# Differential attention beside products: one group of score matmuls per step, two maps in two row halves

## The reference, cut to what matters

```python
q1, q2 = split(h @ w_q)            # each 8 heads x 64, rms_norm per head
kv = rms_norm(h, kv_norm_g) @ w_kv # k1, k2: 8 heads x 64, rms_norm per head; vb: 8 heads x 128
for each head, for each block of queries:
    a = softmax(mask(q1 @ k1.T * scale + bias)) - lam * softmax(mask(q2 @ k2.T * scale + bias))
    o = a @ vb
o = rms_norm(o, sub_g) * (1.0 - lam_init)
h = h + o @ w_o
```

## Time and profile before

| | |
|---|---|
| median of the runs | 2430.57 us |
| profiled execution | 2428.51 us |
| its span, first to last instruction | 2427.2 us |
| PE busy | 2271.9 us (94%), 19314 records |
| PEld busy | 1959.8 us (81%) |
| DVE / ACT / POOL busy | 1460.1 (60%) / 931.3 (38%) / 456.9 us (19%) |
| mean granted TensorE clock | 0.96 |

### The profile page before, as it was taken

One profiled execution on the slowest core, in us unless ns is written; L12 is line 12 of the kernel. 1 busy time (PEld: TensorE's weight loads), 2 busy tenths in 40 slices (PEclk: granted clock), 3 DMA queues, 4 the chain that ended last, 5 costly groups with the idle time before them and its releaser, 6 DMA issues.

```text
span 2427.2 us, 44082 instructions
## 1 busy us (share of the span) xinstructions
PE 2271.9 (94%) x19314; PEld 1959.8 (81%) x19314; DVE 1460.1 (60%) x2342; ACT 931.3 (38%) x1538; POOL 456.9 (19%) x253
## 2 busy tenths in 40 slices
PE   4898999999969999996999999999999998999999
PEld 1677777777757788775689999999877778999987
DVE  3678888888775524377546767533444445776722
ACT  1324444444332525232544343323445545434321
POOL 0444334334302443422220000000000011000000
PEclk7899999999989999896899999999999999999999
DMA  6541011111225234210012332233210012333232
GB/s 235 130 108 45 11 41 41 41 41 41 71 88 160 87 95 142 70 53 26 1 41 86 92 95 89 88 95 115 64 50 27 18 35 88 91 92 93 86 97 73
DMA packets 56831, 184.70 MB, mean 76 GB/s; under 512 B 6816, under 2 KB 6816, under 8 KB 56640
## 3 DMA queue, kind: packets, MB, share of 16 engines
q1 hardware_dynamic: 56640, 181.89, 24.5%
HBM read 174.99 MB, written 6.88 MB: 75 GB/s over the span
## 4 chain that ended last, share of the span: by engine, by line
PE 76%; DVE 15%; ACT 5%; issue 2%; DMA 1%; POOL 0%; SPq 0%; DVEq 0%; POOLq 0%; ACTq 0%
PE PS L532 59%; PE PS L662 4%; DVE ca L1867 3%; PE PS L1106 2%; PE PS L1137 2%; PE PS L857 1%; PE PS L995 1%; PE PS L918 1%; DVE Swk L2220 1%; DVE kx L1935 1%; DVE mx L2216 1%; PE PS L963 1%; PE PS L551 1%; DVE Bf L1941 1%; ACT La L1184 1%
## 5 line engine op out<-in xcount | busy, mean ns | idle before, releaser
L2545 POOL TENSOR_TENSOR wlo<-raw,whi 128x1024 fp32r<-128x1024 f32 (+1 forms) x130 | 304.2, 2341 | 937.2 <-ACT whi L1184 931.1
L532 PE MATMUL PS<-nhi,whi 128*128 128x264 f32 x2064 | 443.9, 296 | 7.1 <-DVE nlo L2108 6.7
L532 PE MATMUL PS<-nlo,whi 128*128 128x264 f32 x2064 | 423.8, 288 | 0.0
L532 PE MATMUL PS<-nhi,wlo 128*128 128x264 f32 x2064 | 421.6, 286 | 0.3 <-POOL wlo L2545 0.3
L1184 ACT ACTIVATE whi<-raw 128x1024 fp32r<-128x1024 f32 (+2 forms) x298 | 302.2, 1015 | 236.6 <-PE PS L532 208.2
L532 PEld LDWEIGHTS PS<-nhi,whi 128*128 128x128 f32 x2064 | 324.2, 191 | 41.1 <-issue 32.9
L532 PEld LDWEIGHTS PS<-nhi,wlo 128*128 128x128 f32 x2064 | 325.0, 191 | 0.5 <-POOL wlo L2545 0.5
L532 PEld LDWEIGHTS PS<-nlo,whi 128*128 128x128 f32 x2064 | 325.2, 191 | 0.0
L1779 DVE TENSOR_TENSOR wlo<-raw,whi 128x1024 fp32r<-128x1024 f32 (+1 forms) x168 | 201.1, 1197 | 168.1 <-ACT whi L1184 167.8
L532 PE MATMUL PS<-hhi,whi 128*128 128x512 f32 x648 | 264.3, 408 | 6.6 <-DVE hlo L1846 6.6
L532 PE MATMUL PS<-hhi,wlo 128*128 128x512 f32 x648 | 258.5, 399 | 1.4 <-POOL wlo L2545 1.4
(11 more groups left out here) (353 smaller groups left out, 3600.6 us busy)
## 6 DMA issues: line engine op xcount, KB each, us to landing
raw<-in_wall SPq DMA_DIRECT2D x290, 512.0 KB, 3.6
raw<-in_wall SPq DMA_DIRECT2D x16, 384.0 KB, 3.1
TZ<-g_rows SPq DMA_DIRECT2D x2, 2112.0 KB, 8.3
raw<-in_wall SPq DMA_DIRECT2D x16, 256.0 KB, 2.6
g_rows<-gsb SPq DMA_DIRECT2D x8, 328.0 KB
xt<-in_xT SPq DMA_DIRECT2D x1, 2048.0 KB, 13.4
o_rows<-os SPq DMA_DIRECT2D x8, 256.0 KB, 2.2
keep<-o_rows SPq DMA_DIRECT2D x8, 256.0 KB, 4.4
```

The source lines that it names most:

```text
L532: q = e.matmul(out, cuts[a][:, k * P:(k + 1) * P], (hi_, lo_)[b][:, kr, lo:lo + w], start=start and k == 0 and a == b == 0, stop=stop and ...
L2545: e.tensor_tensor(wlo[slot[i]][:, w], raw[i % NRAW][:, w], whi[slot[i]][:, w].bitcast(F32), ALU.subtract).then_inc(*up("lo_pool", i))
```

## The change

Four things, in one edit.

1. **A head's two maps share a tile.** The columns of `w_q` and of the keys' part of `w_kv` are put in another order when the inputs are laid out, so that tile h of `qB` and `kB` holds head h: its first map on partitions 0 to 63, its second on 64 to 127. Units of `b_kv` now come as k, v, k, v. `place` is gone; each head is finished by itself.
2. **Both maps of a step are scored in one place**, piece by piece of 136 (or 72) keys, the two maps in turn and so the two row halves in turn. The 528-wide step still scores its maps apart, but with apply and three product steps between them.
3. **The strings.** 16 g instead of 32 come first; `BESIDE` puts scores, apply and turn of a turn next to each other; `AFTER` now holds g as well, since 16 product steps are left for it.
4. **Copies and order on the other engines.** The last 16 keys go to bank 6 beside the whole tiles (bank 7 for the 528-wide step alone); all copies of an even step are ScalarE's and all of an odd step VectorE's. `apply` waits for the copy `b_o` of the apply before it. VectorE inverts the sums of step n-1 ahead of scores(n); ScalarE's order in a turn is scale(n-1), copy(n-3), exponentials(n), PTb copy(n-2). The last q tile is normalized after the first four roundings of the keys' operand (`n2_hi`) instead of before all eight.

```diff
-BESIDE = "agagagagg" "agagagag" "agagagag" "aagaag" "aaaag"
-AFTER = "ag" * 10
+BESIDE = "aagggaagg" "aaaagggg" "aagaaggg" "aaaagg" "aaaag"
+AFTER = "aaggaagg" "aaaagg" "aaagg" "agg" "aagg" "aagg"
...
-            for name in "g" * 32 + 8 * BESIDE + AFTER:
+            for name in "g" * 16 + 8 * BESIDE + AFTER:
...
+        def rest_at(w):
+            return (6, w // P * P) if w < 512 else (7, 256)
...
-                def scores(n, s):
+                def scores(n, maps):
                     h, i = steps[n]
                     q0, nq, w = rows_of(i)
-                    rows, kt = rowsof[h % 2], 4 * s + h // 2
...
-                    scores_free((4, 5) if w > 512 else (4 + s,), ("b_max", n, s))
-                    for out, lo, m_ in halves(w, 4 if w > 512 else 4 + s):
-                        q = e.matmul(out[0:nq, :], qB[rows, kt, q0:q0 + nq], kB[rows, kt, lo:lo + m_], start=True, stop=True)
-                    q.then_inc(*up("b_scores", n, s))
+                    on.wait_ge(*at("qb", h))
+                    on.wait_ge(*at("kb", h))
+                    wide = w > 512
+                    for s in maps:
+                        scores_free((4, 5) if wide else (4 + s,), ("b_max", n, s))
+                    m_ = HT if wide else 136 if w > 144 else min(w, 72)
+                    for lo in range(0, w, m_):
+                        hi_ = min(lo + m_, w)
+                        for s in maps:
+                            out = PS[0:nq, 4 + lo // HT, 0:HT] if wide else PS[0:nq, 4 + s, lo:hi_]
+                            q = e.matmul(out, qB[rowsof[s], h, q0:q0 + nq], kB[rowsof[s], h, lo:hi_], start=True, stop=True)
+                            if hi_ == w:
+                                q.then_inc(*up("b_scores", n, s))
...
                 def apply(n):
...
-                    on.wait_ge(*at("b_PT_end", n))
-                    if w >= P:
-                        on.wait_ge(*at(*turned_by("b", n)))
+                    on.wait_ge(*at(*turned_by("b", n)))
+                    for step in free_o[0]:
+                        on.wait_ge(*at(*step))
...
                 for n in range(N + 6):
+                    wide = n < N and steps[n][1] == 3
                     if n < N:
-                        scores(n, 0)
-                    yield
-                    if n < N:
-                        scores(n, 1)
+                        scores(n, (0,) if wide else (0, 1))
                     yield
                     if 3 <= n <= N + 2:
                         apply(n - 3)
+                    yield
+                    if wide:
+                        scores(n, (1,))
                     yield
                     if 2 <= n <= N + 1:
                         turn(n - 2)
...
+            passed()
             on.wait_ge(*at("unit", count.next - 1))
             for k in range(8):
                 act(nhi[:, k, :], H[:, k, :], ACT.Copy, scale=col("kv_norm_g_2", k)).then_inc(*up("n2_hi", k))
+                if k == 3:
+                    head_norm("qb", 7, qB[:, 7, :], 4, 1.0 / 64, ("qb", 6))
...
+    both = np.arange(1024).reshape(2, 8, 64).transpose(1, 0, 2).reshape(-1)
+    mats["b_q"] = mats["b_q"][:, both]
+    mats["b_kv"] = np.concatenate([mats["b_kv"][:, both], mats["b_kv"][:, 1024:]], axis=1)
```

More of the change, by code:

```diff
@@ L514, in tensor, with product @@
             count = Count()
-            def product(what, hi_, lo_, outs, rhs=None, start=True, stop=True, k0=0, order=None):
+            def product(what, hi_, lo_, outs, rhs=None, start=True, stop=True, k0=0):
                 i = count.take()
@@ L1023, in tensor, with residual @@
             attention("a", 1, qk_a, lambda h, c, m_: Vk[0:m_, c, (h // 4) * P:(h // 4 + 1) * P], lambda h: nothing(), PTa, La)
-            def residual(what, name, hi_, lo_, rhs, n_units=1, order=None, last=False, first=0):
+            def residual(what, name, hi_, lo_, rhs, n_units=1, last=False, first=0):
                 for j in range(8):
@@ L1047, in tensor, with steps_of @@
             e.matmul(PS[:, 4, 0:2], con[0:64, CONE:CONE + 128], lam[0:64, 0:2], start=True, stop=True).then_inc(*up("lam_sum"))
[L1048 to L1051, removed]
+            for h in range(8):
+                normed("b_q", ("qb_raw", h), (lambda k: on.wait_ge(*at("ffn0_n", k))) if h == 0 else None)
+                head_norm("qb", h, blk)
             def made_beside():
-                def steps_of(what, b, hi_, lo_, rhs=None, order=None):
-                    for k, _ in enumerate(product(what, hi_, lo_, halves(T, b), rhs, order=order)):
+                def steps_of(what, b, hi_, lo_, rhs=None):
+                    for k, _ in enumerate(product(what, hi_, lo_, halves(T, b), rhs)):
                         if k == 3 or (k == 1 and what == "b_out"):
@@ L1059, in steps_of, with norm_k, turn_vb @@
                         yield
[L1061 to L1069, removed]
[L1070 to L1079 removed]
+                for h in range(8):
+                    b = banks["kb", h] = pair_of_banks(("kb_log", h))
+                    yield from steps_of("b_kv", b, nhi, nlo, (lambda k: on.wait_ge(*at("n2", k))) if h == 0 else None)
+                    def norm_k(h=h, b=b):
+                        on.wait_ge(*at("kb_sq", h))
+                        sums(sqh, T, b, blk).then_inc(*up("kb_sum", h))
+                    later.append(norm_k)
+                    yield
+                    b = banks["vb", h] = pair_of_banks(("Vb", h))
+                    yield from steps_of("b_kv", b, nhi, nlo)
+                    def turn_vb(h=h, b=b):
+                        on.wait_ge(*at("vb", h))
+                        turn_v(vTb[:, h % 2, :], b).then_inc(*up("vb_turned", h))
+                    later.append(turn_vb)
+                    yield
                 for j in range(8):
                     b = pair_of_banks(("res_b1", j))
[L1082 removed]
+                    yield from steps_of("b_out", b, ohi_b, olo_b, (lambda k: on.wait_ge(*at("ob", k))) if j == 0 else None)
                     yield
@@ L1161, in tensor @@
             run_beside(attend(), made_beside())
-            residual("b_out", "res_b", ohi_b, olo_b, "ob", order=place, first=4)
+            residual("b_out", "res_b", ohi_b, olo_b, "ob", first=4)
             ffn(1, "res_b_n")
@@ L1720, in attend @@
                 for n in range(N + 6):
+                    if 1 <= n <= N:
+                        weights(n - 1)
+                    yield
+                    if 3 <= n <= N + 2:
+                        apply(n - 3)
                     yield
@@ L2504, in attend @@
                     yield
-                    if n < N:
+                    if n < N and not wide:
                         scores(n, 1)
                     yield
+                    if wide:
+                        scores(n, 1)
                     if 1 <= n <= N:
```

212 lines of the change are left out of this document (104 added, 108 removed).

## The result

Four runs of the changed kernel took 2387.79 to 2392.58 us, median 2389.16; the four of the kernel before beside them 2430.77. The ratio is 0.983 (95% interval 0.9813 to 0.9847): 41.6 us faster. The forecast was 2400 with 2391 to 2416 around it.

What follows compares the result with a forecast made beforehand. TensorE was taken as the bound, by how its starts follow one another. Terms -10.1 - 9.4 - 1.5 - 3.3 - 6.5 + 0.3 = -30.5 us gave a median of 2400.1, range 2391 to 2416.

Steps and rivals of the forecast that it cites:

- fewer switches: TensorE in the attention: 7 row-count changes less per head at 0.19 us each, 53 in all, -10.1 us.
- two maps at once: 400-, 272- and 144-wide scores: both maps run side by side in two row halves, 1.17 us per head, -9.4.
- waits: TensorE in the attention: old waits for maximum and copies go, new ones come: -7.7 + 6.2 = -1.5 us.
- clock: Head of 33.45 us with a stretch at 0.50 behind a wait: slow stretch counted as gone, -3.3 (bounds 0 and -3.3).
- end: Behind the last head: the bare chain now runs beside 10 product steps, -6.5 us (bounds -4 and -7).
- start: Ahead of the attention: four roundings before the seventh q head's scaling make the first remainder later, +0.3 us.
- The new wait: 272-wide step: last 16 keys wait for bank 7 until ScalarE's apply copy; 0.8 us in six heads, 4.8.
- The gift of 1.4: First and last head, where the pipeline fills and drains: another 1.4 us of new waits.
- No new waits: Rival for the attention: no new waits and all old ones gone, 2394 us; chance 0.10.
- ScalarE and VectorE did not become the bound: Rival: their queues become the bound, two more waits of 0.9 per head, 14 us, time 2414; chance 0.20.
- the halves ran side by side: Rival said they would not, with pieces of 136 columns: the 9.4 falls away, time 2413; chance 0.08.
- nothing was slower: Rival said slower: TensorE stands for an apply copy in each of 40 steps, 2436 at 0.9 us; chance 0.03.

Runs made afterwards that it cites:

- run 1: Changed kernel with whole-width scores, both maps scored from the lower half of the partitions; median 2393.87 us, stretch 269.36 (whole-width alone 260.80).
- run 7: Changed kernel with 32 product steps ahead of the attention and none beside its last turns; median 2396.17 us, 7.0 more, stretch 265.02.
- run 4: Changed kernel with the last 16 keys of every turn back in bank 7; median 2397.30 us, stretch 271.90, 10.2 longer.
- run 5: Kernel before with only the last 16 keys moved to bank 6 and a turn's copies on one engine; median 2428.54 us against 2429.80.
- Run 9: Changed kernel with ScalarE's copy of the 16-wide apply ahead of the scaling of the 400-wide map; median 2387.18 us, stretch 259.16.
- run 10: Changed kernel with the 16-row remainder ahead of an apply's whole tiles, except the 144-wide apply; median 2385.99 us, stretch 257.66.
- run 2: Changed kernel with one whole-width score matmul per map instead of pieces; median 2384.68 us, stretch 260.80.
- run 3: Changed kernel with all score pieces of the first map ahead of all of the second; median 2388.73 us, stretch 262.29, 0.6 more.

## Why the prediction was right in its parts and wrong in its sum

| term | forecast | measured | from |
|---|---|---|---|
| fewer switches | -10.1 | -10.1 | the count measured (places where rows change in two heads: 56 before, 42 after), the price 0.19 as forecast; see below |
| two maps at once | -9.4 | -10.2 | 27.30 (run 1) less 26.03, per head |
| waits | -1.5 | -9.4 | starts of PE, 12.0 before, 2.6 after |
| clock | -3.3 | -3.0 | third head 33.45, less the 30.50 of a head with the same wait |
| end | -6.5 | -7.1 | what is left, with the errors of the other rows; by covering it 3.3 (run 7) |
| start | +0.3 | +0.2 | from the last sum of `b_q` to the keys' first product 5.47 before, 5.65 after; ahead of the stretch |
| sum | -30.5 | -39.8 | stretch 301.46 to 261.69, without the start |

**The step that failed** is "-7.7 + 6.2 = -1.5", 7.9 of the 9.3 us missed, in both of its halves.

*What went.* I took 7.7 from the column of waits. That column counts idle time, and PE is idle only when the matmul before has drained. By starts (the gap to the matmul before, less the smallest gap of the same kinds in either kernel) the attention lost 12.0: 7.2 for the second wide map (6.7 as idle), 1.4 before applies (1.0), 2.35 in 22 last transposes behind the copy of the apply ahead of them, and 0.96 at seven 16-wide scores (0.35 behind a product instead of 0.21). Of the last two the column has nothing. The 16-wide scores start 0.05 behind the end of ScalarE's reading of the head's sum (`sqb`), which lies in their banks. The forecast named the move of the last 16 keys to bank 6 as part of the change and gave it no price at all. Runs 4 and 5 show that it has one: 0.2 to 0.5 us a head in the kernel before, 0.8 to 1.1 in the changed one.

*What came.* The new wait is where I put it and ends as I said. The timeline after, fifth head:

```profile
1870.13 0.71 DVE L2158 TENSOR_TENSOR kB<-PS,rstd 128x528 f32<-128x528 f32 x1 [0.19 <-PE PS L535]
...
1870.47 1.04 ACT L1191 ACTIVATE whi<-raw 128x1024 fp32r<-128x1024 f32 x1
...
1871.55 1.23 DVE L1784 TENSOR_TENSOR wlo<-raw,whi 128x1024 fp32r<-128x1024 f32 x1 [0.71 <-ACT whi L1191]
...
1872.89 0.63 ACT L1191 ACTIVATE Lb<-Lb,small 128x400 f32<-128x400 f32 x1 [0.84 <-DVE small L2487]
...
1873.42 0.16 ACT L1191 ACTIVATE oT<-PS 128x16 f32<-128x16 f32 x1
...
1873.64 0.28 PE L1130 MATMUL PS<-con,Lb 128*16 128x128 f32 x1 [0.47 <-ACT oT L1191]
```

`whi`, `wlo`, inversion, scaling, copy, transpose: 3.5 us from the end of the k unit, where VectorE takes it. Run 9 takes the wait away. But it occurs in four heads instead of six, 0.64, 0.38, 0.64 and 0.37 (2.0 in all, 4.8 forecast), and filling and draining the pipeline cost 0.55, not 1.4. The chain was overcounted: `whi` begins 0.34 us after the k unit ends and not 0.6 (0.35 in the third head). In the fourth and sixth head it is 0.09 and 0.08 (1843.82 against 1843.73 in the fourth), and the wait is shorter by the same 0.25; in the second it begins ahead of the unit's end (1790.45 against 1791.06), and there is no wait. The gift of 1.4 rested on no row.

**The rest.** *Switches*: the count of 7 per head holds. The price is not measured by itself; it is what is left of a head. The fourth head before takes 30.16, the seventh after 26.03; of the 4.13 between them 1.47 are waits by starts and 1.27 the two maps, and 1.4 remain for 7 switches, where 1.33 was forecast. That is 0.19 to 0.20 each; the other three, of run 10, were worth 0.09 to 0.19. *Two maps*: right, and without the order rule of the Trainium skill ("strict FIFO, no reordering"; TensorE: Matmul & The Clock Gate, "The mechanism"). As I applied it, it does not hold between halves here: in run 2 the upper half starts ahead of one pass of the lower that stands before it, in run 3 ahead of three. The belief behind the pieces, that only neighbours overlap, was wrong as well. *Clock*: that I called it chance in part was too cautious. The stretch comes at the same place in both profiles of the kernel before and in run 5, which has the same waits and two more such stretches behind them; of the profiles with the wide map's wait taken away or shortened none has it there (run 4, with a wait of 1.9 us of another kind, has a short one behind it). That the waits cause it is supported by these, not proven for every wait: the one of 1.3 us in the fifth head had no such end in either profile of the kernel before, and one of 1.5 us there had one in run 5. *End*: the sum is right, the reason half so. Of 7.1 us the product steps beside it are worth 3.3 (run 7). The other half came without them: from the first apply of the bare chain to the first product behind its sum go 8.3 us before (2007.34 to 2015.61) and 5.7 in run 7, of which PE is idle 2.9 and 2.1, and the chain before lies partly in a stretch at 0.50 (2010.5 to 2017.4). The wait for `olo_b` is gone in run 7, the slow products are not, as its stretch at 0.50 shows. How much of this is the order of the parts and how much the clock no run separates.

**The rivals.** "No new waits", 2394, lay nearer, with a chance of 0.10; its size was still short, because it too took the waits at 7.7. ScalarE and VectorE did not become the bound, the halves ran side by side, nothing was slower. The range failed on its low side: it let the new waits vary and the old ones not.

## What to carry to other kernels

Read the price of a wait from the starts of the waiting engine against the smallest gap of the same pair of instructions, not from its idle column: on TensorE here 22 waits of 0.05 to 0.17 us behind another matmul, 2.35 us in all, showed as none. Give every edit in the diff a term, a change of buffer too. And where few rows of the stationary side change between neighbours (64, 16, 128), sort them: each change taken away gave 0.09 to 0.19 us (run 10).

## What the runs showed of the hardware that was not expected

- Matmuls in two row halves overlap fully (starts 0.007 us apart) without alternating in the program: behind two fp32 matmuls of 136 columns (four passes) of the other half the next one still starts 0.014 us after the first pass, behind three (six passes) 0.34 us after it, with the third. In both cases it starts ahead of three passes.
- A stretch repeats far better than the whole: the heads of the kernel before agree within 0.05 us between its two profiles, while its runs spread over 2423 to 2434 us.
- Back in one half, two 400-wide scores took 1.54 us; side by side 0.87.
